# The first projection: 16 blocks by fp32 products from feature rows, 18 blocks whole and wide

## The chip, the cores and the metric

One core of one Trainium2 chip. The kernel is one launch, and its time is device microseconds (us) from start to end; of several runs the median is taken. The engines are named as in the profile: PE (TensorE matmuls), PEld (its weight loads), DVE (VectorE), ACT (ScalarE), POOL (GpSimd), SP (the queue that issues the loads).

## The reference, cut to what matters

Two transformer blocks follow each other on x of 256 tokens by 2048 features, in float32. The change touches only the start of the first:

```python
mod = silu(c) @ w_ada + b_ada                    # w_ada 2048 x 12288
sh_a, sc_a, gt_a, sh_f, sc_f, gt_f = split(mod, 6)
h = rmsnorm(x, norm_mix) * (1.0 + sc_a) + sh_a   # shift: columns 0:2048, scale: 2048:4096 of w_ada
p = h @ w_in                                     # 2048 x 9296
c_q, c_kv, k_pe, q_g, k_g, v_g, z, b_logit, a_logit, gate_logits = split_cols(p)
```

The branches behind p are a latent attention (MLA: c_q, c_kv and k_pe, with an RMS norm on c_q and c_kv), a gated delta rule (q_g, k_g and v_g pass a causal convolution of four taps with silu, then an l2 norm; b_logit and a_logit give its gates), and sigmoid gates. A second block without modulation follows.

## The kernel before, in words

The matrices have features in partitions: h is 16 tiles of 128 features by 256 tokens. A product of 128 features of the input with 128 of the output is a *tile*; there are 6864. Weights come in *units* of 512 KB (128 x 1024, eight tiles). Each unit of a linear layer (kind "L") is split in two: ACT rounds it to fp32r (`hi`, L519), DVE takes the rest (`lo`, L659); h is split likewise (H1). A *narrow* tile is three fp32r products of 256 columns (L354 to L356: hi by hi, hi by lo, lo by hi). A *wide* tile is two: hi by both halves of h in one product of 512 columns, lo by hi in one of 256 (L348 to L352); its bank holds two sums, which ACT and DVE add when they take it out (`raw_sum`, with L523 and L671).

A unit of w_ada (kind "A", 192 of them) is multiplied on DVE by c and added to an accumulator (L651, L655), one unit of 128 rows of c by 1024 columns after the other; after 16 units, PE sums over partitions (`mod_sum`, L361). The first 64 units, four *groups* of 16, give shift and scale for four tiles of h each. So tiles 0 to 3 of h exist after 16 units, 4 to 7 after 32, and so on.

A single function, `walk`, is run once per engine, and fixes the order of the work on each. `kinds` is the order of the units in the load queue; there are 13 slots for them at first (5 RAW, 8 EARLY, the latter in room that H2 takes later), and 5 after unit `early`. Work beside the tiles is put in generators with `later(gen, lag, gap)`: they start `lag` tiles on and give one step every `gap` tiles. `force()` runs one step of each when a bank or result is missing. PSUM's 8 banks are two rings, `lbank` (3) and `mbank` (5).

The first projection has 34 blocks of output (`CBLK`: c_q, c_kv, k_pe and the gate logits b, a; `Q03`, `Q47`: 24 of q, k, v), each over 16 tiles of h, 544 narrow tiles. It runs in four eras: `partial` takes all 34 blocks over tiles 0 to 3 of h, then over 4 to 7, then over 8 to 11, and the last loop (`LATE`) over 12 to 15. What an era leaves is kept in `part` (B1 and B2). ACT copies out the first era; in the second and third, every second block is added by DVE (`combine`, L709) and every second one by ACT and POOL (L523, L932); the last is added by DVE. `kinds` puts 17 L units and 16 A units in each of the first three eras.

Behind and beside the last era come: `cnorm` (the norms of c_q, c_kv), `qkv_chain` (the taps L760, tanh L534 and product L713 of 24 blocks), `l2norm(0)` (eight sums on PE, L403, and four spreads L408), then `ups(0)` to `ups(7)` (the latent attention's up projections, 112 narrow tiles, with the attention of 8 heads in steps beside them), then 16 blocks of gate b, gate a, z, and so on, all wide. `gdn()` (L824 to L872), the delta rule in four rounds, is put up ahead of `ups` and waits for `l2norm(0)`; it gives one step each 4 tiles, beside whatever tiles there are.

Of the kernel before, what the change touches and what calls it, by code (L numbers as in the profile page):

```python
# [12 lines left out]
ERA = 17  # L13
HAND = 4
TAPS = 4
# [178 lines left out]
SIGNALS = ("tile", "hi", "lo", "ada", "mod_p", "mod_v", "pre_a", "pre_v", "ev_a", "ev_v", "ev_g", "ev_p",  # L194
           "st_a", "st_v", "st_g", "st_p", "ad_v", "l2_a", "l2_v", "l2_p", "gd_p", "gd_a", "gd_v", "at_p", "at_a",
           "at_v", "at_g", "cv_a", "cv_v", "cv_p", "spin")
LOADS = tuple(f"raw{i}" for i in range(NRAW + NEARLY)) + tuple(f"bias{i}" for i in range(4)) + ("cols", "consts", "x", "pos", "x2", "out")


def program(nc, xT, pos, cols_d, consts_d, wada, wst, bias_d, out, log):  # L200
# [8 lines left out]
    with ctx:  # L209
# [71 lines left out]
        RQ, RV = SC[:, 0:2], SC[:, 2:4]  # L281
        R12, R1, ACC2 = B3[:, 0, :], B3[:, 1, :], B3[:, 2, :]
# [8 lines left out]
        ACC = (ADA[:, :], B2[:, 20:24, :].rearrange("p a t -> p (a t)"))  # L291
# [8 lines left out]
        def sync(e):  # L300
# [9 lines left out]
            def load_x(i):  # L310
                e.dma_start(X[:, 4 * i:4 * i + 4, :], xT[:, 4 * i:4 * i + 4, :]).then_inc(S["x"], 16)

            def load_x2(i, free):
                q.wait_ge(free)
                e.dma_start(X[:, 4 * i:4 * i + 4, :], xT[:, 4 * i:4 * i + 4, :]).then_inc(S["x2"], 16)
# [24 lines left out]
        def tensor(e):  # L340
            q = Engine(e, S)

            def tile(u, i, bk, H, k, wide, second, first, last, lo, h, free):
# [160 lines left out]
            walk(dict(tile=tile, mod_sum=mod_sum, spin=spin, stat_add=stat_add, stat_sum=stat_sum, acc2_sum=acc2_sum, rope_turn=rope_turn, ba_turn=ba_turn,  # L504
# [5 lines left out]
        def scalar(e):  # L510
            q = Engine(e, S)

            def c_sigmoid(cols):
                q.wait_ge(cols)
                e.activation(SC[:, 16:32], col("c", 0, 16), ACT.Sigmoid).then_inc(S["pre_a"], 1)

# [113 lines left out]
            walk(dict(c_sigmoid=c_sigmoid, hi=hi, copy_sum=copy_sum, split_hi=split_hi, tanh=tanh, sigmoid=sigmoid, square=square,  # L630
# [3 lines left out]
        def vector(e):  # L634
# [13 lines left out]

            def ada_first(acc, slot, raw, c, free):
                q.wait_ge(raw, c, free)  # L650
                e.tensor_scalar(acc, raw_at(slot), SC[:, 0:1], None, mult).then_inc(S["ada"], 1)  # L651
# [12 lines left out]

            def mod_add2(g, bk, summed, cols):
                q.wait_ge(summed, cols)
                e.tensor_tensor(m2h(MOD[:, 0:32])[:, :, 4 * g:4 * g + 4], m2h(bk[:, 0:8]), m2h(col("b_ada", 0, 32))[:, :, 4 * g:4 * g + 4], add).then_inc(S["mod_v"], 1)
# [230 lines left out]
            walk(dict(c_silu=c_silu, halve=halve, norm_product=norm_product, ada_first=ada_first, ada_next=ada_next, lo=lo, mod_add=mod_add, mod_add2=mod_add2, sum_halves=sum_halves,  # L898
# [37 lines left out]
        def walk(mine, log=None):  # L936
            w = Walk(mine)
            do, load, later, need, now = w.do, w.load, w.later, w.need, w.now
            st = {"load": 0, "proc": 0, "na": 0, "nl": 0, "la": 0, "ll": 0}
            tv = Ring(w, [TV[:, i, :] for i in range(4)])  # L940
# [4 lines left out]
            kinds = ["A"] * 16  # L945
            for g in range(GROUPS - 1):
                put = 0
                for i in range(ERA):
                    due = min(16, max(0, -(-16 * (i - 1) // (ERA - 5))))
                    kinds += ["L"] + ["A"] * (due - put)  # L950
                    put = due
            put = 16 * GROUPS
            late_at = len(kinds) - 16
            for i in range(ERA * (GROUPS - 1), N_TILES // 8):
# [3 lines left out]
            lin_at = [i for i, k in enumerate(kinds) if k == "L"]  # L958
            early = 16 * GROUPS + ERA * (GROUPS - 1)
# [5 lines left out]
            group_tok = [None] * GROUPS  # L965
# [5 lines left out]
            def load_next():  # L971
# [5 lines left out]
                if kinds[s] == "A":  # L977
# [15 lines left out]
            def proc_next():  # L993
                s = st["proc"]
                slot = slot_of(s)
                if kinds[s] == "A":
# [3 lines left out]
                    acc = ACC[j % 2] if j < GROUPS else ACC[0]  # L1000
                    if t == 0:
                        before = j - 2 if j < GROUPS else j - 1
# [1400 lines left out]
```

## Time and profile before

| | |
|---|---|
| runs | 2845.52 us median of 3 (2835.41 to 2852.19) |
| the profiled execution | 2841.27 us, span 2839.3 us, mean granted clock 0.989 |
| PE, DVE, ACT, POOL busy | 2723.7, 2033.5, 1359.1, 207.0 us |
| loaded | 560.39 MB read, 199 GB/s on average |

A stage's busy times are read beside its length: the engine that is nearly full there sets it. PE's ends are modelled, so that a matmul of 0.28 us can start 0.12 us after the one before it: what a product costs in a stream is the distance of starts. An fp32 product stands in the profile as two records.

### The profile page before, as it was taken

Reading aid. Unit: us, or ns where it says so; the run is one execution under the profiler, and the core shown is the slowest. Engines: PE = TensorE matmul, PEld = TensorE weight load, DVE = VectorE, ACT = ScalarE, POOL = GpSimd, SP = SyncE. Lnnn points to the kernel's source line nnn. Section 1 sums busy time; section 2 is a strip of 40 time slices with the busy share of each in tenths; the row PEclk is TensorE's granted clock in tenths of the full one; section 3 lists DMA queues with packets and bytes.
Section 4 is the critical chain, followed back from the end, with each engine's and each line's share of the span. In section 5 each row is a group of like instructions: output and inputs, shape, how many; then the busy total and the mean of one; then the engine's idle time right before and its main releaser. Section 6 shows DMA issues by size and latency. Waiting matters only on the chain.

```text
span 2839.3 us, 43991 instructions
## 1 busy us (share of the span) xinstructions
PE 2723.7 (96%) x17404; PEld 2453.9 (86%) x17404; DVE 2033.5 (72%) x2989; ACT 1359.1 (48%) x2169; POOL 207.0 (7%) x180
## 2 busy tenths in 40 slices
PE   6988899999999999999999999999999999999997
PEld 6888888998899788888888889998888888888886
DVE  7898787777796886555555679996567566565665
ACT  4445753433444544444444554466554444444454
POOL 0231000000002000000000180111110000000001
PEclk9999999999999999999999999999999999999999
DMA  9864355566787686555555554544445555555553
GB/s 391 315 234 134 104 179 192 195 213 203 255 304 254 224 301 217 189 189 190 189 188 191 186 173 163 180 166 138 157 134 178 191 187 191 186 190 189 186 192 126
DMA packets 158461, 565.37 MB, mean 199 GB/s; under 512 B 17584, under 2 KB 21936, under 8 KB 158256
## 3 DMA queue, kind: packets, MB, share of 16 engines
q1 hardware_dynamic: 158256, 562.56, 58.4%
q8 instruction: 138, 2.26, 0.3%
q14 instruction: 67, 0.55, 0.1%
HBM read 560.39 MB, written 2.10 MB: 198 GB/s over the span
## 4 chain that ended last, share of the span: by engine, by line
PE 84%; DVE 10%; ACT 3%; issue 2%; DMA 1%; SPq 0%; POOL 0%; DVEq 0%; ACTq 0%; POOLq 0%
PE BK L351 20%; PE BK L349 20%; PE BK L352 10%; PE BK L348 10%; PE BK L354 6%; PE BK L356 5%; PE BK L355 5%; DVE LO L659 3%; PE BK L436 2%; ACT HI L519 1%; DVE ADA L655 1%; DVE B L878 1%; DVE B L709 1%; PE BK L361 1%; DVE TV L760 1%
## 5 line engine op out<-in xcount | busy, mean ns | idle before, releaser
L519 ACT ACTIVATE HI<-RAW 128x1024 fp32r<-128x1024 f32 x825 | 875.0, 1061 | 1229.8 <-PE BK L349 846.8
L659 DVE TENSOR_TENSOR LO<-RAW,HI 128x1024 fp32r<-128x1024 f32 x825 | 1017.0, 1233 | 376.8 <-ACT HI L519 374.4
L351 PE MATMUL BK<-H,HI 128*128 128x512 f32 x2528 | 1011.2, 402 | 8.9 <-DVE LO L659 8.5
L349 PE MATMUL BK<-H,HI 128*128 128x512 f32 x2496 | 985.7, 396 | 0.0
L352 PE MATMUL BK<-H,LO 128*128 128x256 f32 x2528 | 703.0, 278 | 0.0
L348 PE MATMUL BK<-H,LO 128*128 128x256 f32 x2496 | 698.4, 280 | 0.4 <-DVE H L705 0.2
L354 PE MATMUL BK<-H,HI 128*128 128x256 f32 x1840 | 547.8, 298 | 35.2 <-DVE B L709 16.8
L348 PEld LDWEIGHTS BK<-H,LO 128*128 128x128 f32 x2496 | 469.8, 188 | 111.5 <-DVE H L705 2.0
L352 PEld LDWEIGHTS BK<-H,LO 128*128 128x128 f32 x2528 | 477.1, 189 | 100.1 <-issue 0.7
L355 PE MATMUL BK<-H,HI 128*128 128x256 f32 x1840 | 525.8, 286 | 0.0
L356 PE MATMUL BK<-H,LO 128*128 128x256 f32 x1840 | 525.5, 286 | 0.0
L351 PEld LDWEIGHTS BK<-H,HI 128*128 128x128 f32 x2528 | 481.3, 190 | 18.4 <-DVE LO L659 10.0
L349 PEld LDWEIGHTS BK<-H,HI 128*128 128x128 f32 x2496 | 469.3, 188 | 3.8
L354 PEld LDWEIGHTS BK<-H,HI 128*128 128x128 f32 x1840 | 357.6, 194 | 51.8 <-DVE B L709 18.5
L355 PEld LDWEIGHTS BK<-H,HI 128*128 128x128 f32 x1840 | 358.1, 195 | 2.1
L356 PEld LDWEIGHTS BK<-H,LO 128*128 128x128 f32 x1840 | 357.7, 194 | 0.0
L914 POOL TENSOR_TENSOR SQ<-SQ,B 128x256 f32<-128x256 f32 x63 | 81.2, 1288 | 1491.5 <-ACT B L542 1487.8
L655 DVE SCALAR_TENSOR_TENSOR ADA<-RAW,SC,ADA 128x1024 f32<-128x1024 f32 x133 | 171.0, 1286 | 2.8 <-DMA RAW<-wada_dram 1.9
L705 DVE TENSOR_TENSOR H<-TV,H 128x256 fp32r<-128x256 f32 x124 | 52.4, 424 | 165.8 <-ACT H L530 165.6
L671 DVE TENSOR_TENSOR TV<-BK,TE 128x256 f32<-128x256 f32 x255 | 106.2, 418 | 36.9 <-ACT TE L523 36.8
L523 ACT ACTIVATE TE<-BK 128x256 f32<-128x256 f32 x352 | 128.2, 366 | 1.2 <-PE BK L349 0.8
L878 DVE SCALAR_TENSOR_TENSOR B<-B,CO 128x256 f32<-128x256 f32 x240 | 110.3, 520 | 1.8 <-ACT B L602 1.8
(248 smaller groups left out, 1878.8 us busy)
## 6 DMA issues: line engine op xcount, KB each, us to landing
RAW<-wst_dram SPq DMA_DIRECT2D x825, 512.0 KB, 3.3
RAW<-wada_dram SPq DMA_DIRECT2D x155, 512.0 KB, 4.5
EARLY<-wada_dram SPq DMA_DIRECT2D x37, 512.0 KB, 8.9
EARLY<-wst_dram SPq DMA_DIRECT2D x33, 512.0 KB, 7.7
X<-xT_dram SPq DMA_DIRECT2D x8, 512.0 KB, 9.2
B<-bias_dram SPq DMA_DIRECT2D x32, 128.0 KB, 3.3
out_dram<-X SPq DMA_DIRECT2D x3, 512.0 KB, 2.7
CN<-consts_dram SPq DMA_DIRECT2D x1, 900.0 KB, 9.7
```

The costliest lines, as they stand in the source:

```text
L348: e.matmul(bk[:, 256:512], ll, H[:, k, 0:256], start=False, stop=False, skip_group_check=True)
L349: e.matmul(bk[:, :], hh, H[:, k, :], start=False, stop=last, skip_group_check=True).then_inc(S["tile"], 1)
L351: e.matmul(bk[:, :], hh, H[:, k, :], start=first, stop=False, skip_group_check=True)
L352: e.matmul(bk[:, 256:512], ll, H[:, k, 0:256], start=False, stop=last, skip_group_check=True).then_inc(S["tile"], 1)
L354: e.matmul(bk[:, 0:256], hh, H[:, k, 0:256], start=first, stop=False, skip_group_check=True)
L355: e.matmul(bk[:, 0:256], hh, H[:, k, 256:512], start=False, stop=False, skip_group_check=True)
L356: e.matmul(bk[:, 0:256], ll, H[:, k, 0:256], start=False, stop=last, skip_group_check=True).then_inc(S["tile"], 1)
L519: e.activation(HI[:, u % NHL, :], raw_at(slot), ACT.Copy).then_inc(S["hi"], 1)
L523: e.activation(dst, src, ACT.Copy).then_inc(S["ev_a"], 1)
L655: e.scalar_tensor_tensor(acc, raw_at(slot), SC[:, t:t + 1], acc, mult, add).then_inc(S["ada"], 1)
L659: e.tensor_tensor(LO[:, u % NHL, :], raw_at(slot), HI[:, u % NHL, :].bitcast(f32), sub).then_inc(S["lo"], 1)
L878: e.scalar_tensor_tensor(CA[j], UP[:, j, i:i + 256], CO[:, o + i:o + i + 1], CA[j], mult, add).then_inc(S["cv_v"], 1)
```

## The change

The first 64 units of w_ada are laid out the other way round: a unit (kind "R") holds 128 *output features* in partitions by 1024 of the 2048 values of c; four such units (shift and scale, two halves each) are a *feature row*. c is spread to all partitions once (`c_spread`, `c_row`: CR). DVE multiplies the unit by CR in place, ACT sums it over its free axis. After four units shift and scale of one tile of h are there (`mod_row`), and `modulated` makes that tile in float32 (HF, in B2); x is scaled by its norm ahead of that (`x_scaled`). The tile is also split into H1, as before.

The first 16 of the 34 blocks (`FIRST`: CBLK and six of Q03) are accumulated over the 16 rows in all 8 banks, two blocks to a bank, by one fp32 product per tile (`direct`), straight from the loaded unit (kind "D") without hi and lo. The order of loads is R for two rows, then per row two D units and the four R units of the row two on. When row 15 is done, the 16 halves are copied out, and the 18 other blocks (`REST`) run whole over 16 tiles of h as wide tiles. There are no partial sums, no `part_add` on POOL, and no `mod_sum` for these 64 units. `cnorm`, k_pe and the logits are thus put up first; the tap chain starts 24 tiles into REST, at a step each 6 tiles (`TAPS`, 4 before); `scalars` steps each 4 tiles (8 before); `l2norm(0)` starts 64 tiles in. x's squares are four instructions of 1024 columns, each waiting for its own quarter of x, and c and x are loaded ahead of all units.

The core of the diff:

```diff
-ERA = 17
+ROWS_AHEAD = 2
+DIRECT = 16
-TAPS = 4
+TAPS = 6
+            def direct(slot, i, bk, o, k, last, raw, h, free):
+                q.wait_ge(raw, h, free)
+                e.matmul(bk[:, o:o + 256], raw_at(slot)[:, 128 * i:128 * i + 128], HF[k], start=(k == 0 and o == 0), stop=last,
+                         skip_group_check=True).then_inc(S["tile"], 1)
+            def unit_sum(slot, c, product):
+                q.wait_ge(product)
+                e.activation(raw_at(slot), raw_at(slot), ACT.Copy, accum_out=SM[:, c:c + 1]).then_inc(S["ada_a"], 1)
+            def unit_product(slot, half, raw, row):
+                q.wait_ge(raw, row)
+                e.tensor_tensor(raw_at(slot), raw_at(slot), CR[:, 1024 * half:1024 * half + 1024], mult).then_inc(S["ada"], 1)
-            kinds = ["A"] * 16
-            for g in range(GROUPS - 1):
...
+            kinds = ["R"] * (4 * ROWS_AHEAD)
+            for i in range(16):
+                kinds += ["D"] * (DIRECT // 8) + ["R"] * (4 if i + ROWS_AHEAD < 16 else 0)
...
+            spin(10)
+            def row_end(j, sums):
+                x = do("x_scaled", "ad_v", j, rs_tok[0], tk_x[j // 4])
+                m = do("mod_row", "mod_v", j, sums, tk_cols, n=3)
+                yield
+                hf_tok[j] = do("modulated", "ev_a", j, m, x)
+                yield
+                h_tok[j] = yield from split(H1, j, HF[j], hf_tok[j])
+                row_done.pop(0)
...
-            for k in range(0, 12, 4):
-                partial(range(k, k + 4))
...
+            for r in range(16):
+                if r + ROWS_AHEAD < 16 + 1 and r > 0:
+                    for i in range(4):
+                        row_unit(r + 1, i)
+                while hf_tok[r] is None:
+                    next(row_done[0], None)
+                direct_row(r)
...
-            later(scalars(), 16, 8)
-            later(l2norm(0), 0, 6)
-            later(qkv_chain(), 0, TAPS)
+            for b, n in enumerate(FIRST):
+                own, bk, _ = held[b // 2]
+                later(ev_first(n)(bk[:, 256 * (b % 2):256 * (b % 2) + 256], done_tok[b | 1], (own, b % 2)))
+            later(scalars(), 16, 4)
+            later(l2norm(0), 64, 6)
+            later(qkv_chain(), 24, TAPS)
+            for n in REST:
+                run(block(H1, h_tok, 0, "w_in", 0, n, ev_qkv(n - 9, True), wide=True))
```

`row_unit(j, i)` is the product and the sum of one unit, and a step of the last row's `row_end`; `direct_row(r)` is 16 `direct` tiles from two units.

## Rows read from the trace of the kernel before

**Rows 1.** the page: busy time per engine over the span

```profile
PE 2723.7 (96%) x17404; PEld 2453.9 (86%) x17404; DVE 2033.5 (72%) x2989; ACT 1359.1 (48%) x2169; POOL 207.0 (7%) x180
```

**Rows 2.** windows by stage: length, busy per engine (instructions), clock, DMA share, GB/s

```profile
39.90:100.00 60.10, 58.73 (x443) 55.38 (x444) 46.16 (x50) 30.12 (x57) 0.00 (x0) 0.97 0.90 351
100.00:200.00 100.00, 88.90 (x701) 85.87 (x699) 95.02 (x109) 39.47 (x61) 37.26 (x28) 0.98 0.84 305
200.00:240.00 40.00, 35.46 (x278) 34.51 (x278) 30.42 (x51) 22.10 (x37) 12.69 (x12) 0.97 0.28 93
240.00:287.00 47.00, 40.73 (x300) 37.18 (x300) 42.20 (x91) 26.51 (x45) 0.00 (x0) 0.99 0.40 132
287.00:358.50 71.50, 62.71 (x455) 58.59 (x455) 56.28 (x127) 52.87 (x139) 0.00 (x0) 0.98 0.30 99
...
378.00:450.00 72.00, 70.52 (x452) 62.97 (x451) 58.66 (x80) 32.98 (x56) 0.00 (x0) 1.00 0.59 198
```

**Rows 3.** the timeline to the first tile: start us, us, engine, line

```profile
17.28 9.80 PE L366 MATMUL BK<-TE,CN 128*128 128x256 f32 x32 [17.28 <-ACT TE L542]
...
39.89 0.55 PE L354 MATMUL BK<-H,HI 128*128 128x256 f32 x1 [2.13 <-DVE H L701]
```

**Rows 4.** two narrow tiles in steady running, the timeline

```profile
43.69 0.28 PE L354 MATMUL BK<-H,HI 128*128 128x256 f32 x1
...
44.05 0.28 PE L354 MATMUL BK<-H,HI 128*128 128x256 f32 x1
```

**Rows 5.** one pair of wide tiles and the next, the timeline of PE

```profile
1600.13 0.40 PE L351 MATMUL BK<-H,HI 128*128 128x512 f32 x1
...
1600.83 0.39 PE L351 MATMUL BK<-H,HI 128*128 128x512 f32 x1
```

**Rows 6.** the chain of work: start us, us, line, count

```profile
83.00 1.68 PE BK L361 x16
...
420.33 0.86 PE BK L408 x4
```

**Rows 7.** groups of instructions by form, from 0 to 520 us

```profile
L659 DVE TENSOR_TENSOR LO<-RAW,HI 128x1024 fp32r<-128x1024 f32 x85 | 107.9, 1271 | 5.8 <-ACT HI L519 5.8
L519 ACT ACTIVATE HI<-RAW 128x1024 fp32r<-128x1024 f32 x85 | 89.9, 1058 | 134.7 <-PE BK L349 74.3 <-PE BK L356 54.1 <-DMA RAW<-wst_dram 4.3
...
L932 POOL TENSOR_TENSOR B<-B,TE 128x256 f32<-128x256 f32 x34 | 43.7, 1286 | 176.2 <-ACT TE L523 176.2
...
L709 DVE TENSOR_TENSOR B<-BK,B 128x256 f32<-128x256 f32 x60 | 24.8, 415 | 0.0
```

**Rows 8.** the timeline of DVE, tap chain beside the last era

```profile
268.32 1.22 DVE L659 TENSOR_TENSOR LO<-RAW,HI 128x1024 fp32r<-128x1024 f32 x1
...
269.79 1.51 DVE L760 SCALAR_TENSOR_TENSOR TV<-B,CO,TV 128x255 f32<-128x255 f32 x3
...
271.79 0.43 DVE L713 SCALAR_TENSOR_TENSOR B<-B,TV 128x256 f32<-128x256 f32 x1
272.13 1.22 DVE L659 TENSOR_TENSOR LO<-RAW,HI 128x1024 fp32r<-128x1024 f32 x1
...
286.44 0.42 DVE L709 TENSOR_TENSOR B<-BK,B 128x256 f32<-128x256 f32 x1
```

**Rows 9.** the timeline of DVE while POOL adds

```profile
105.54 1.75 DVE L659 TENSOR_TENSOR LO<-RAW,HI 128x1024 fp32r<-128x1024 f32 x1
```

**Rows 10.** windows: two stretches of the first loads

```profile
0.00:20.00 20.00, 2.72 (x7) 2.18 (x7) 7.91 (x11) 3.36 (x7) 0.19 (x4) 1.00 0.91 346
...
60.00:80.00 20.00, 19.42 (x151) 18.20 (x151) 17.55 (x15) 9.71 (x19) 0.00 (x0) 1.00 1.02 407
```

**Rows 11.** lines 760 and 828 (first of gdn): durations, first and last start

```profile
L760 DVE SCALAR_TENSOR_TENSOR TV<-B,CO,TV x72: 466/482/486, 262.0 to 376.4; 128x255 f32<-128x255 f32 x24, 128x254 f32<-128x254 f32 x24, 128x253 f32<-128x253 f32 x24
...
L828 DVE TENSOR_TENSOR B<-CN,B x4: 628/656/685, 378.3 to 636.7; 128x512 f32<-128x512 f32 x4
```

**Rows 12.** the timeline of ACT: an activation with a sum read out

```profile
298.80 0.19 ACT L584 ACTIVATION_READ_ACCUMULATOR B<-B,SC 128x1 f32 x1
```

More of the change, by code:

```diff
@@ new lines, in walk, with row_unit @@
+            spin(10)
+            row_done = []
+            hf_tok = [None] * 16
+            def row_unit(j, i):
+                s, slot = st["proc"], slot_of(st["proc"])
+                v = do("unit_product", "ada", slot, i % 2, raw(s), cr_tok)
+                raw_free[slot] = do("unit_sum", "ada_a", slot, 4 * j + i, v)
+                st["proc"] += 1
+                while load_next():
+                    pass
+                for f in list(row_done):
+                    next(f, None)
+                if i == 3:
+                    row_done.append(row_end(j, raw_free[slot]))
@@ L1213, in rotary @@
                     yield
-                for _ in range(16):
+                for _ in range(7):
                     yield
@@ new lines, in walk, with __init__, release @@
+            REST = (CBLK + Q03 + Q47)[DIRECT:]
+            later(rotary(), 8, 8)
+            class Halves:
+                def __init__(self, ring, i):
+                    self.ring, self.i, self.used = ring, i, []
+                def release(self, half, *signals):
+                    self.used.append(list(signals))
+                    if len(self.used) == 2:
+                        self.ring.release(self.i, *self.used)
+            held = []
+            for b in range(DIRECT // 2):
+                ring = lbank if lbank.idle else mbank
+                bi, bk, fr = ring.get()
+                held.append((Halves(ring, bi), bk, fr))
@@ new lines, in walk, with direct_row @@
+            hi_tok.update({u: None for u in range(2 * DIRECT)})
+            done_tok = [None] * DIRECT
+            def direct_row(r):
+                for g in range(DIRECT // 8):
+                    s = lin_at[w.tile // 8]
+                    slot = slot_of(s)
+                    for i in range(8):
+                        b = 8 * g + i
+                        own, bk, fr = held[b // 2]
+                        w.tile += 1
+                        if log is not None:
+                            log.append(("w_in", r, FIRST[b]))
+                        done_tok[b] = do("direct", "tile", slot, i, bk, 256 * (b % 2), r, r == 15, raw(s), need(hf_tok, r), fr if r == 0 else None)
+                    raw_free[slot] = done_tok[b]
+                    assert st["proc"] == s
+                    st["proc"] += 1
+                    while load_next():
+                        pass
+                    w.flush()
@@ new lines, in walk @@
+            for r in range(16):
+                if r + ROWS_AHEAD < 16 + 1 and r > 0:
+                    for i in range(4):
+                        row_unit(r + 1, i)
+                while hf_tok[r] is None:
+                    next(row_done[0], None)
+                direct_row(r)
+            while row_done:
+                next(row_done[0], None)
+            r_last = ("ada", w.count["ada"])
+            p1_end = [("tile", w.tile), h_tok[15], r_last]
+            feed(w.tile // 8 + 2)
@@ L1284, in f @@
                 def f(bk, tok, own):
-                    half, hk = half_of(j)
-                    cq_tok[j] = combine(CQ[j], bk, half, add, tok, own, hk, x_used)
+                    cq_tok[j] = copy_out(CQ[j], bk, tok, own, x_used)
                     yield
+                    while j > 3 and SQS[0].done is None:
+                        yield
                     if j == 4:
-                        while SQS[0].done is None:
-                            w.force()
                         SQS[1] = Stats(*SQS[0].before, SQS[0].done)
```

186 lines of the change are left out of this document (78 added, 108 removed).

## The prediction

> **What bounds the kernel now.** The page comes first: PE is busy 96% of the span, DVE 72% [rows 1]. So time can be won only where PE idles or where its work shrinks. The windows by stage show where it idles. Its first tile starts at 39.9 us [rows 3]. From there to 287 us, the end of the first projection (DVE takes its last sum out at 286.4 [rows 8]), PE is busy 223.8 of 247.1 us, and then 62.7 of the 71.5 us of the `ups` [rows 2]. From 378 us on it is nearly full (70.5 of 72). Busy time hides part of it, since each matmul's modelled end runs past the next start. Counted by starts, a narrow tile takes 0.36 us [rows 4], and 544 of them 196 us. With some 8 us of sums beside them (three `mod_sum` at 1.68 us [rows 6] and small things), 204 us of work take 247: 43 us are lost, after 40 us of start.
>
> What fills the other engines there: DVE is busy 95 of the 100 us from 100 to 200, and 42.2 of 47 from 240 to 287 [rows 2]. In the second and third era a `lo` takes 1.75 us while POOL adds [rows 9], against a mean of 1.27 and 1.22 alone [rows 7, 8]. In the last era the period is 3.81 us (from `lo` to `lo` [rows 8]) for eight narrow tiles, 2.9 us of PE: DVE sets the pace, with a `lo`, two sums and one block's taps.
>
> **The start.** Before, c and one group of 16 units must be there ahead of the first tile. After, c, x (2.1 MB) and eight units are needed, with two chains. x's quarters land by about 9 us; c's spread is 16 short fp32 products and four copies, to about 13 us. The 16 sums of squares took 9.8 us [rows 3], so norms are ready at about 22 to 24 us. Row 0 then needs two units' products of row 1 on DVE in front of `modulated` on ACT (the queues are in order), some 4 us. I put the first `direct` tile at 28.5 us (25 to 35).
>
> **The direct stage, 16 rows.** PE: an fp32 product of 256 columns with a new stationary each time took 0.43 us (two products, 0.86 for four records [rows 6]). A row of 16 is 6.9 us, 16 rows 110 us, where the same 256 tiles cost 92 us as narrow ones: the change adds 18 us of PE work here. Loads: six units of 0.524 MB per row at 407 GB/s [rows 10] are 7.7 us. DVE: four products like a `lo` without POOL, whose starts lie 1.14 us apart behind it, about 4.6 us, and some 1.2 us of small steps. ACT: four copies of 1.06 [rows 7] with a sum read out (0.19 more [rows 12]), about 5 us, and two steps on a tile of h, 0.8. So loads set the pace at 7.7 us a row, and PE follows at 90%. By 20 us 6.9 MB are in (346 GB/s [rows 10]); the first unit of row 13 ends the first 48.2 MB, at 20 + 41.3/0.407 = 121 us. Behind it come one D unit of row 13, four R units of row 15 and four D units, all in by 133 us, so that rows 13 to 15 go nearly at PE's pace: 121 + 3 x 6.9 = 142 us. By PE alone it would be 28.5 + 110 = 138.5. I take 143, with the change of banks (two ACT copies ahead of the first bank, mostly while row 15 still runs).
>
> The Trainium skill (FP8 and Floating Point Precision, TensorE Precision Notes) says true fp32 takes four passes, against the three products of a narrow tile. By that rule a tile would be 4/3 of 0.36, an estimate of 0.48 us, 123 us in all, and PE as slow as the loads. The row shows 0.43, so the trace is a little kinder, and the sum uses the row.
>
> **The wide stage.** A pair of wide tiles takes 0.70 us [rows 5], so 288 tiles are 100.8 us. Beside them PE has `l2norm(0)`: 8 row sums at 0.43 and four spreads at 0.86, 6.9 us, by the same row of 0.86 [rows 6], and about 2.5 us for norms, k_pe and logits. DVE: 36 `lo` at 1.14 (41 us), 22 blocks of taps, tanh and product at 1.77 by starts (1.43 and 0.34; 39 us), 18 sums of halves at about 0.34 (6 us), norms, rotary, scalars, l2 rows about 17 us (an estimate: some 45 steps of 0.3 to 0.45 us, by the starts of L709 and L713 [rows 8]): 103 of 110 us. That is tight but does not bind alone: 12 tiles a block of taps are 4.2 us of PE, against 3.75 of DVE. At the front 16 copies, eight squares, tables and splits crowd on ACT beside `hi`; HI and LO hold three units, 8.4 us. For this crowd and the tight stretch I allow 10 us of stalls (4 to 20). The end is 143 + 101 + 9.4 + 10 = 263 us, against 287: 24 us won.
>
> **Behind it.** `l2norm(0)` lay behind 287 before, since the taps ran to 376.4 [rows 11]; now it is done: 6.9 us of PE work less. DVE loses 17 of 24 blocks of taps there (17 x 1.77 = 30 us), and ACT their two passes each. But `gdn`, whose first decay step stood at 378.3 [rows 11], can start with the `ups`, and brings its own DVE steps and in-order waits. The work of `gdn` isn't smaller, only earlier. Of the 8.8 us in which PE idles there [rows 2] I take half as won: 4 us (0 to 9, or a loss of 10 if it crowds). The hundreds of us after are full for PE before, and I take nothing from them.
>
> The first 64 units cost DVE the same (1.2 us each by either operation), the D units cost neither `hi` nor `lo`, and `part_add` leaves POOL: nothing on the path beyond what is counted. The angles for k_pe run in the direct stage, where DVE has 1.9 us free a row. SP issues in order and waits for slots: 13 slots are 2 rows ahead, 15 us, and a D unit is freed at most 7 us after it is used, so no wait binds unless PE falls behind.
>
> The sum: 24 + 6.9 + 4 = 35 us. Against the profiled execution's own time, 2841.3, that gives 2806; it lies 4 us below the median of the runs shown, so against 2845.5 the figure is 2810. Between them I give **2809**.
>
> **Rivals.**
> *The delta rule crowds the attention (0.17).* Both want `mbank`, DVE and PE in order. For it: in the `ups` DVE had 56.3 and ACT 52.9 of 71.5 us [rows 2], and PE waits there for single softmax steps. Against it: 30 us of taps go. If each of some 28 steps costs PE 0.6 us, 17 us are lost: gain 18, 2827 us.
> *DVE or ACT paces the wide stage (0.10).* If the tap chain runs at 5 us a block rather than 4.2, 22 blocks cost 17 us: 2827 too. For it: 3.81 us periods in the last era came with only 90% busy DVE [rows 2, 8].
> *Loads slower than 407 GB/s in the direct stage (0.04).* At 358 the 41.3 MB take 115 us and not 101, 14 us more: 2823. Against it stand the 20 us windows at 407 [rows 10]. The Trainium skill (DMA: Bandwidth & Descriptors, Specifications) gives a limit of about 358 GB/s per core from HBM; by that rule the time is this rival's, but the trace disagrees, with 407.
> *More is won (0.09).* If both stages stall less (3 us) and the `ups` win all 9, and later waits for the delta rule's end shrink by 5: gain 52, 2794.
> *Slower (0.08).* PE's clock falls to 1.2 GHz in the direct stage, where each row leaves PE waiting for loads. Then a product is 0.86 us and a row 13.8; 16 rows are 220 us and the kernel about 80 us slower than forecast, 2885. It decides from 35 / 0.43 = 81 products, about five rows of 16, at the lower level. Against it: with waits in every 8 tiles from 100 to 200 us, PE kept 0.98 of the clock [rows 2].
> *The forecast itself (0.52):* first direct tile 25 to 32, its end 138 to 148, wide stage 113 to 125 long, gain 26 to 44.
>
> **How the numbers follow.** Own range of the likeliest: 2800 to 2819. The range takes in the losses of rivals one to three and half of "more": 2790 to 2834; outside lie 0.08 slower, a few hundredths of the crowding cases together, and the best ones. A change of 0.5% (14 us) is about what a measurement tells from none. Faster by over that: 0.52 + 0.09 + three quarters of 0.31 (18 us hardly clears 14) = 0.84, less a little for causes not thought of: 0.80. Same: 0.11. Slower: 0.09.
>
> **What the profile after would show.** Right: POOL almost empty before 150 us; `direct` about 0.43 us a start, rows 7.7 us apart, 400 GB/s until about 130 us; the last at 140 to 148; no narrow tile until about 263; wide pairs 0.70 us apart with `lo` never late; gdn's first L828-like step within 15 us of the first `ups`. Wrong: a granted clock under 0.9 between 30 and 145; direct products more than 0.5 us apart; ACT in front of `hi` for more than 8 us behind the direct stage; PE busy below 85% in the `ups`. The sum fails most easily in the wide stage's stalls and in what the `ups` give back.

## The result, and the profile after

The kernel after takes 2826.69 us (median of 7 runs, 2822.4 to 2828.04), the kernel before 2845.52 (7 runs, 2835.41 to 2852.19): a ratio of 0.9936, 95% interval 0.9923 to 0.9948. That is 18.8 us faster, about half of the 36 us forecast. The profiled execution took 2822.49 us with a span of 2820.7.

The page, busy time per engine over the span. Against [rows 1] POOL lost 48 us, DVE 60, PE only 3:

```profile
PE 2720.4 (96%) x16824; PEld 2429.0 (86%) x16824; DVE 1973.0 (70%) x2951; ACT 1387.3 (49%) x2235; POOL 158.7 (6%) x146
```

The timeline of PE in the direct stage: start, length, line, and in brackets the idle time before and what ended it. This answers to [rows 3] and to the pace in [rows 2]:

```profile
25.66 9.85 PE L364 MATMUL BK<-B,EARLY 128*128 128x256 f32 x32 [5.04 <-ACT B L538]
35.35 7.07 PE L364 MATMUL BK<-B,RAW 128*128 128x256 f32 x32
...
102.99 7.17 PE L364 MATMUL BK<-B,RAW 128*128 128x256 f32 x32 [0.51 <-DMA RAW<-wst_dram]
110.67 7.17 PE L364 MATMUL BK<-B,EARLY 128*128 128x256 f32 x32 [0.51 <-DMA EARLY<-wst_dram]
118.35 7.17 PE L364 MATMUL BK<-B,RAW 128*128 128x256 f32 x32 [0.51 <-DMA RAW<-wst_dram]
126.31 7.17 PE L364 MATMUL BK<-B,EARLY 128*128 128x256 f32 x32 [0.78 <-DMA EARLY<-wst_dram]
133.99 1.35 PE L364 MATMUL BK<-B,RAW 128*128 128x256 f32 x5 [0.51 <-DMA RAW<-wst_dram]
```

A row is 32 records, 16 products. Without a wait the next row starts 6.91 us on (35.35 to 42.26), 0.43 us a product; with the wait for the load it is 7.68 (102.99 to 110.67 to 118.35). Both are the forecast's numbers. The first row shows the lower clock (0.50 from 26 to 30 us), 9.7 us for 16 products. That seems to cost nothing later, since from 95 us on every row waits for its load.

Windows by stage: start and end, length, busy time of PE, PEld, DVE, ACT and POOL with instructions, PE's clock, DMA share, GB/s:

```profile
30.00:125.00 95.00, 90.77 (x406) 77.87 (x405) 74.20 (x121) 65.05 (x124) 0.00 (x0) 0.98 1.03 409
...
148.00:180.00 32.00, 21.85 (x109) 17.96 (x107) 18.70 (x44) 21.32 (x45) 5.19 (x6) 0.84 0.33 115
180.00:220.00 40.00, 37.92 (x214) 32.61 (x215) 36.80 (x66) 24.05 (x44) 0.00 (x0) 1.00 0.56 182
220.00:250.00 30.00, 28.76 (x160) 24.64 (x158) 23.23 (x40) 21.08 (x39) 0.00 (x0) 1.00 0.47 157
250.00:276.00 26.00, 25.34 (x142) 22.17 (x143) 23.46 (x44) 12.61 (x21) 0.00 (x0) 1.00 0.48 149
276.00:365.00 89.00, 79.74 (x616) 75.19 (x615) 54.66 (x110) 44.36 (x115) 0.00 (x0) 0.98 0.30 96
```

The hole is in one place: of the 32 us from 148 on PE is busy 21.85, at 0.84 of the clock. Three markers tell where the gain lies. The first narrow tile (the end of the first projection) starts at 275.8 us, against 286.8 before: 11.0 won of the 24 forecast. The reload of x, far behind, is issued at 767.2 against 784.1: 17.0 won, so 5.9 between the markers, where 6.9 + 4 were forecast. The span is 18.6 shorter, so 1.6 came behind. The last two are small beside what the same kernel varies by: run again (e0 below), it took 493.0 us between the markers where the run here took 491.3 (before: 497.3), and 2055.4 behind the reload where the run here took 2053.5 (before: 2055.2). So 4 to 6 us were won between the markers, and nothing that can be told from none behind them.

What PE waited for from 147.7 to 275.8 (line, releaser: us in total, times, longest):

```profile
PE BK L413 <- DVE B L816: 8.5, 1, 8.5
PE BK L355 <- DVE LO L703: 2.3, 3, 0.9
PE BK L385 <- POOL SQ L954: 1.4, 2, 1.2
PE BK L423 <- DVE RS L765: 1.3, 1, 1.3
PE BK L418 <- ACT TE L603: 0.6, 1, 0.6
```

14.1 us, of which 8.5 is a single wait: PE's queue holds the gates' running sum (L413, two tiny products), which needs DVE's L816. Why L816 is late stands in the timelines of ACT and of DVE:

```profile
156.68 1.04 ACT L542 ACTIVATE HI<-RAW 128x1024 fp32r<-128x1024 f32 x1
...
160.52 0.42 ACT L553 ACTIVATE H<-TV 128x256 fp32r<-128x256 f32 x1 [1.73 <-DVE TV L753]
161.83 0.42 ACT L553 ACTIVATE H<-TV 128x256 fp32r<-128x256 f32 x1 [0.89 <-DVE TV L753]
...
164.44 0.42 ACT L553 ACTIVATE H<-TV 128x256 fp32r<-128x256 f32 x1 [0.89 <-DVE TV L753]
164.87 1.28 ACT L572 ACT_TABLE_LOAD   x1
166.16 1.28 ACT L586 ACT_TABLE_LOAD   x1
...
167.69 1.28 ACT L589 ACT_TABLE_LOAD   x1
...
169.45 1.04 ACT L542 ACTIVATE HI<-RAW 128x1024 fp32r<-128x1024 f32 x1
```

```profile
161.32 0.48 DVE L753 SCALAR_TENSOR_TENSOR TV<-X,CO,RS 128x256 f32<-128x256 f32 x1
162.28 0.43 DVE L745 TENSOR_TENSOR H<-TV,H 128x256 fp32r<-128x256 f32 x1 [0.48 <-ACT H L553]
162.62 0.48 DVE L753 SCALAR_TENSOR_TENSOR TV<-X,CO,RS 128x256 f32<-128x256 f32 x1
...
169.78 0.17 DVE L816 SCALAR_TENSOR_TENSOR B<-B 128x16 f32<-128x16 f32 x1
```

`cnorm(1)` needs the last piece of `cnorm(0)` (`need(H2_tok, 3)`), and so all four pieces are issued in one burst. Each goes DVE, ACT, DVE (L753, L553, L745) with a wait at each hand-over, 1.30 us a piece; behind them ACT loads three tables. After the `hi` (L542) that starts at 156.68 the next starts at 169.45, 12.8 us on.

PE behind that wait:

```profile
170.01 0.61 PE L413 MATMUL BK<-B,CN 128*128 128x16 f32 x2 [8.47 <-DVE B L816]
...
171.89 0.63 PE L353 MATMUL BK<-H,HI 128*128 128x512 f32 x1
...
173.17 0.63 PE L353 MATMUL BK<-H,HI 128*128 128x512 f32 x1
...
175.18 0.40 PE L353 MATMUL BK<-H,HI 128*128 128x512 f32 x1
...
175.87 0.40 PE L353 MATMUL BK<-H,HI 128*128 128x512 f32 x1
```

A pair of wide tiles takes 1.28 us until about 174.5 (the level of 1.2 GHz) and 0.69 to 0.70 from then on: some 1.6 us more.

### The profile page after: what moved, and what is told of

The parts are those of the page before. It is cut to its first block, busy times and chain, and to the rows that moved or that the text cites. A ratio compares the mean times of both kernels' runs of the same rounds, so it can differ in the third digit from the quotient of the medians.

```text
span 2820.7 us, 42647 instructions
## 1 busy us (share of the span) xinstructions
PE 2720.4 (96%) x16824; PEld 2429.0 (86%) x16824; DVE 1973.0 (70%) x2951; ACT 1387.3 (49%) x2235; POOL 158.7 (6%) x146
## 4 chain that ended last, share of the span: by engine, by line
PE 83%; DVE 9%; ACT 4%; DMA 2%; issue 1%; SPq 0%; POOL 0%; ACTq 0%; DVEq 0%
PE BK L355 21%; PE BK L353 21%; PE BK L356 10%; PE BK L352 10%; PE BK L358 4%; PE BK L360 4%; PE BK L359 4%; DVE LO L703 2%; PE BK L451 2%; DVE B L918 2%; PE BK L364 2%; ACT HI L542 1%; DMA RAW<-wst_dram 1%; DMA RAW<-wada_dram 1%; PE BK L376 0%
## 5 line engine op out<-in xcount | busy, mean ns | idle before, releaser
L542 ACT ACTIVATE HI<-RAW 128x1024 fp32r<-128x1024 f32 x826 | 875.6, 1060 | 1202.2 <-PE BK L353 828.6
L355 PE MATMUL BK<-H,HI 128*128 128x512 f32 x2672 | 1070.0, 402 | 12.2 <-DVE LO L703 11.6
L353 PE MATMUL BK<-H,HI 128*128 128x512 f32 x2640 | 1042.1, 396 | 0.0
L356 PE MATMUL BK<-H,LO 128*128 128x256 f32 x2672 | 743.2, 278 | 0.0
L352 PE MATMUL BK<-H,LO 128*128 128x256 f32 x2640 | 738.3, 280 | 0.4 <-DVE H L745 0.2
L352 PEld LDWEIGHTS BK<-H,LO 128*128 128x128 f32 x2640 | 496.7, 188 | 118.2 <-DVE H L745 2.0
L356 PEld LDWEIGHTS BK<-H,LO 128*128 128x128 f32 x2672 | 504.0, 189 | 106.5 <-issue 0.7
L355 PEld LDWEIGHTS BK<-H,HI 128*128 128x128 f32 x2672 | 508.1, 190 | 23.6 <-DVE LO L703 14.9
L353 PEld LDWEIGHTS BK<-H,HI 128*128 128x128 f32 x2640 | 496.0, 188 | 3.7
L358 PE MATMUL BK<-H,HI 128*128 128x256 f32 x1296 | 383.5, 296 | 13.9 <-DVE LO L703 7.8
L359 PE MATMUL BK<-H,HI 128*128 128x256 f32 x1296 | 368.1, 284 | 0.0
L360 PE MATMUL BK<-H,LO 128*128 128x256 f32 x1296 | 368.1, 284 | 0.0
L358 PEld LDWEIGHTS BK<-H,HI 128*128 128x128 f32 x1296 | 249.7, 193 | 20.5 <-DVE LO L703 12.9
L359 PEld LDWEIGHTS BK<-H,HI 128*128 128x128 f32 x1296 | 249.8, 193 | 2.3 <-issue 0.2
L360 PEld LDWEIGHTS BK<-H,LO 128*128 128x128 f32 x1296 | 249.6, 193 | 0.0
L745 DVE TENSOR_TENSOR H<-TV,H 128x256 fp32r<-128x256 f32 x124 | 52.3, 424 | 164.2 <-ACT H L553 164.2
L699 DVE SCALAR_TENSOR_TENSOR ADA<-RAW,SC,ADA 128x1024 f32<-128x1024 f32 x120 | 154.0, 1283 | 0.8 <-DMA RAW<-wada_dram 0.6
L546 ACT ACTIVATE TE<-BK 128x256 f32<-128x256 f32 x336 | 122.1, 366 | 1.2 <-PE BK L353 0.8
## 6 DMA issues: line engine op xcount, KB each, us to landing
B<-bias_dram SPq DMA_DIRECT2D x32, 128.0 KB, 3.3
```

Of the source, the lines that this page charges most:

```text
L352: e.matmul(bk[:, 256:512], ll, H[:, k, 0:256], start=False, stop=False, skip_group_check=True)
L353: e.matmul(bk[:, :], hh, H[:, k, :], start=False, stop=last, skip_group_check=True).then_inc(S["tile"], 1)
L355: e.matmul(bk[:, :], hh, H[:, k, :], start=first, stop=False, skip_group_check=True)
L356: e.matmul(bk[:, 256:512], ll, H[:, k, 0:256], start=False, stop=last, skip_group_check=True).then_inc(S["tile"], 1)
L542: e.activation(HI[:, u % NHL, :], raw_at(slot), ACT.Copy).then_inc(S["hi"], 1)
L546: e.activation(dst, src, ACT.Copy).then_inc(S["ev_a"], 1)
```

## The experiments

All ran beside the kernel before on the same chip; "stage" is the length of the wide stage in the profiled run, from its first tile to the first narrow tile; "T1" is the start of that narrow tile, and "reload" the issue of x's reload. The stage is the steadier measure: the direct stage ends between 147.5 and 149.5 us from run to run (141.1 in e8), and T1 carries that along. Where nothing in the stage was changed (the kernel after, e0, e3, e8) it is 128.0 or 128.1 us, in e7 and e11 126.3 and 125.6, in e12 and e16 105.1 twice.

| kernel | us, median | ratio (95%) | stage | T1 | reload |
|---|---|---|---|---|---|
| e0 the kernel after again | 2826.72 | 0.9944 (0.9928 to 0.996) | 128.0 | 277.4 | 770.5 |
| e1 scalars 16, 8 | 2825.76 | 0.9943 (0.9928 to 0.9959) | 128.1 | 276.0 | 769.8 |
| e2 scalars 64, 8 | 2823.99 | 0.9941 (0.9927 to 0.9954) | 129.7 | 278.2 | 768.1 |
| e4 TAPS 4 | 2829.86 | 0.9962 (0.9947 to 0.9977) | 134.7 | 282.2 | 771.3 |
| e5 the old order of side work | 2845.51 | 1.0013 (1.0004 to 1.0022) | 146.4 | 294.6 | 787.6 |
| e6 norm's pieces spread | 2822.7 | 0.9931 (0.9918 to 0.9945) | 125.6 | 274.6 | 766.3 |
| e7 e6 and scalars 64, 8 | 2822.43 | 0.993 (0.9918 to 0.9942) | 126.3 | 274.8 | 764.4 |
| e8 less to load | 2818.89 | 0.9917 (0.9899 to 0.9935) | 128.0 | 269.0 | 759.5 |
| e3 gdn at `ups(6)` | 2821.07 | 0.9925 (0.9908 to 0.9941) | 128.0 | 276.4 | 764.1 |
| e9 chain from tile 0 | 2827.65 | 0.9946 (0.9927 to 0.9965) | 132.1 | 280.2 | 769.3 |
| e10 e7, chain behind the stage | 2816.5 | 0.9914 (0.9891 to 0.9937) | 104.4 | 252.7 | 759.3 |
| e11 e7 and e3 | 2817.43 | 0.9911 (0.9895 to 0.9928) | 125.6 | 274.3 | 760.5 |
| e12 e10, chain from tile 96 | 2807.36 | 0.9874 (0.9856 to 0.9892) | 105.1 | 252.8 | 747.6 |
| e13 e7, chain from tile 64 | 2808.58 | 0.9884 (0.9866 to 0.9902) | 116.4 | 264.4 | 751.2 |
| e14 e9 and TAPS 4 | 2842.18 | 1.0002 (0.9992 to 1.0011) | 143.6 | 291.3 | 783.8 |
| e15 chain from tile 96 alone | 2824.55 | 0.9938 (0.9924 to 0.9951) | 119.8 | 267.8 | 767.7 |
| e16 e12 and e3 | 2807.86 | 0.9878 (0.9864 to 0.9892) | 105.1 | 253.6 | 750.8 |
| e17 e6, chain from tile 96 | 2819.59 | 0.9925 (0.9911 to 0.9938) | 112.5 | 260.3 | 763.7 |

**Is it one wait? (e1, e2)**

```diff
-            later(scalars(), 16, 4)
+            later(scalars(), 16, 8)    # e1; 64, 8 in e2
```

> The steps of the gates' scalars 8 tiles apart instead of 4 (as in the kernel before), nothing else. Theory A (PE stands still because the cumulating matmul is put up ahead of its inputs: the DVE and ACT queues are still busy with the norms): the matmul comes 12 tiles, 4.2 us, later in PE's order, so the wait shrinks from 8.5 to 4 to 5 us, with less time at the lower clock behind it; 4 to 6 us faster than e0. Rival B (DVE and ACT are the bound of this stretch, PE's wait is only where it shows): the wait moves to the weights' lo and the time stays within 1.5 us of e0.

> The scalars start 64 tiles into the wide stage instead of 16, 8 tiles a step. Theory A: the 8.5 us wait and the 1.8 us at the lower clock behind it go whole, 9 to 11 us faster than e0, less up to 2 us for two or three more activation table loads of 1.28 us in the tap chain. Rival B: within 2 us of e0, with waits for lo in its place.

The same view of PE's waits, of e1 (first two lines) and of e2 (last two), each from 147.7 to 276 us:

```profile
PE BK L413 <- DVE B L816: 5.6, 1, 5.6
PE BK L355 <- DVE LO L703: 3.6, 1, 3.6
```

```profile
PE BK L355 <- DVE LO L703: 7.3, 4, 3.5
PE BK L413 <- DVE B L816: 3.0, 1, 3.0
```

8.5 + 2.3 became 5.6 + 3.6, and then 3.0 + 7.3. The wait for the gates goes to `lo`, and the stage stays (128.1 and 129.7 us, against 128.0 in e0); the kernel is 1.0 and 2.7 us from e0, near what rival B expects. With the matmul moved away, the burst still keeps ACT from `hi`. "An early matmul in PE's queue" falls as the cause: it is only where PE notices.

**The gap of the chain, and the old order (e4, e5, e9, e14)**

```diff
-TAPS = 6
+TAPS = 4                           # e4, e5, e14
-            later(scalars(), 16, 4)
-            later(l2norm(0), 64, 6)
-            later(qkv_chain(), 24, TAPS)
+            later(scalars(), 16, 8)            # e5
+            later(l2norm(0), 0, 6)             # e5
+            later(qkv_chain(), 0, TAPS)        # e5, e9, e14
```

> The tap chain gives a step each 4 tiles instead of 6; it ends some 100 tiles earlier. If DVE has the room that I worked out (3.75 us of work for each 4.2 us of PE), it has not at this pace: 1.0 lo, one block's taps and half a sum in 2.8 us of PE is 3.1 us of DVE, so the wide stage is 5 to 10 us longer for two thirds of its length and then shorter, the sum within 4 us of e0. Rival (the pace of the taps sets the delta rule's start): faster by 3 us or more, with the delta rule's first step before 276 us.

> The order of the side work as the kernel before has it (taps at once and each 4 tiles, l2 norm at once, scalars each 8 tiles), on the new scheme. Theory: the taps then share DVE and ACT with the norms from the first tile, the start of the wide stage is worse; the first narrow tile comes at 280 to 290 us instead of 276, and the whole is 3 to 10 us slower than the changed kernel. Rival (the order behind the direct stage doesn't matter, only the work does): within 2 us.

> The kernel after, with the tap chain started at the first wide tile instead of 24 tiles in (one number; gap of 6 kept). The kernel with the whole old order of side work took 2845.5 and its wide stage ended 19 us later. Theory 'tanh passes between the norms' passes: each change between tanh and another table costs ACT 1.28 us, and DVE's in-order queue waits for ACT, so that lo is late': the chain's start is most of it; ACT loads 12 or more tables up to the end of the stage (7 in the kernel after), lo is waited for by 10 us or more, the first narrow tile at 284 to 292, kernel 2835 to 2842. Rival 'the gap of the chain (4 against 6) is most of it': the first narrow tile at 276 to 281, kernel 2827 to 2831.

> The kernel after with the chain at the first wide tile and a gap of 4 (the two together; each alone moved the first narrow tile by 4 to 6 us, and with the old places of scalars and l2norm(0) too it was 19). If the two just add: first narrow tile 286, kernel 2832 to 2836. If it is the two together that make the 19 us: 292 to 296, kernel 2840 to 2846.

e5 missed by far: with the old order the new direct stage is worth nothing (2845.5, T1 294.6). e4 came in as expected. e9 did not bear its theory out: T1 and the whole time lie in its rival's ranges, and PE waits once, 12.8 us, for L816, and not for `lo`. e14 lies near the second of its two cases. Alone, the gap makes the stage 6.6 us longer and the chain's start 4.0; together 15.5 (e14). So they don't add. From 147 to 276 us ACT loads 7 tables in the kernel after, 11 in e9, 12 in e14 and 14 in e5, each 1.28 us: tanh and the norms' functions take turns. But their number does not set the stage's length: e4 loads 7 in 134.7 us, e6 and e7 below load 10 and 11 in 125.6 and 126.3. In e5 DVE waits longest for one tanh, with five table loads ahead of it on ACT between 176.9 and 185.2 us:

```profile
185.60 0.43 DVE L753 SCALAR_TENSOR_TENSOR B<-B,TV 128x256 f32<-128x256 f32 x1 [6.15 <-ACT B L557]
185.94 1.22 DVE L703 TENSOR_TENSOR LO<-RAW,HI 128x1024 fp32r<-128x1024 f32 x1
```

The `lo` behind it in DVE's queue comes late. PE's two long waits lie on either side: 9.2 us until 177.2, for the `lo` before this one, which stood behind the norm's four pieces, a block of taps and a tanh; and 6.6 us until 189.3, for L816.

**Spread the burst (e6, e7)**

```diff
             def cnorm(half):
...
+                while half and H2_tok[3] is None:
+                    yield
```

> The norm of c_kv waits with a yield for the norm of c_q instead of forcing its steps. Theory C: that force puts the eight steps of c_q's norm (DVE, ACT, DVE, four times 1.3 us) in one burst in front of hi and lo, 158 to 166 us, and the three units of split weights run dry; spread out, ACT and DVE reach hi again after one step, the wait of the cumulating matmul shrinks to under 4 us, and the first narrow tile comes 4 to 8 us earlier. Rival (the table loads and the gates' own chain, not the burst, set it): first narrow tile within 2 us of 276.

> The same wait with a yield, and the scalars 64 tiles in, 8 tiles a step. Theory C: neither burst nor early matmul; PE waits under 4 us between 150 and 200 us, first narrow tile at 264 to 268 us, the whole 8 to 12 us faster than the changed kernel. Rival (DVE's share of the wide stage is the bound, 102 of 128 us with its round trips): at best 3 us faster.

The clock from 148 to 180 us is 1.00 in both, where it was 0.84, and PE is busy 27.4 and 29.6 of these 32 us, not 21.9. But the next 40 us pay for it (35.4 and 32.2, not 37.9), where taps, norms and scalars meet: the stage is 2.5 and 1.8 us shorter. The kernel is 4 us faster than e0, but its ratio (0.9931, 0.993) is within the interval of the kernel after's (0.9923 to 0.9948), so a gain in the whole time isn't shown. Both expectations missed: T1 was to come 4 us earlier or more. PE's waits in e7:

```profile
PE BK L413 <- DVE B L816: 6.0, 1, 6.0
PE BK L355 <- DVE LO L703: 3.9, 5, 1.8
PE BK L423 <- DVE RS L765: 1.3, 1, 1.3
```

**Take the chain away (e10), bring it back later (e12, e13, e15, e17)**

```diff
-            later(l2norm(0), 64, 6)
-            later(qkv_chain(), 24, TAPS)
+            later(l2norm(0), 320, 6)           # e10, e12
+            later(qkv_chain(), 288, TAPS)      # e10; 96 in e12, e15, e17; 64 in e13
```

e10, e12 and e13 stand on e7, e17 on e6, e15 on the kernel after.

> From the kernel with the norm's waits and late scalars (2822.4): the tap chain starts 288 tiles into the wide blocks, behind all of them, and the l2 norm's sums 320 tiles in, so that the wide stage has no taps, no tanh and no l2 norm. Theory 'DVE's and ACT's side steps in order set the wide stage': with 22 blocks of taps (39 us of DVE) gone, lo is never late behind the norms, the 7 us of l2norm(0) on PE are gone too, and the first narrow tile is at 275 - 7 - 6 = 262 (258 to 265). Rival 'the front alone (norms, scalars) holds the stage up': 267 to 269, by the l2 norm's 7 us alone. The kernel as a whole: the taps go beside the ups and the delta rule starts late, so that its end (hg_done) may be waited for: 2822 to 2850; I say 2835.

> The kernel with the taps behind the wide stage (2816.5, first narrow tile at 252.7), with the chain started 96 tiles into the wide blocks, so that 16 of its 24 blocks lie in the wide stage, but none beside the norms and the scalars. Theory 'it is the chain beside the norms and scalars that costs, not the chain': the wide stage stays within 3 us of 252.7 (252 to 256), and with 16 blocks of taps gone from the ups the kernel takes 2806 to 2815. Rival 'each block of taps beside wide tiles costs PE 0.8 us or so': first narrow tile at 264 to 268, kernel 2816 to 2822.

> The kernel with the norm's waits and late scalars (2822.4, first narrow tile 274.8), with one number changed: the chain starts 64 tiles in, not 24. The scalars still start at 64, so the two overlap. By the theory that the overlap with the norms and scalars costs, the part of it that lies with the norms goes: first narrow tile at 262 to 268, kernel 2812 to 2818. By the rival (taps cost wherever they lie): 1 to 3 us won by the blocks that leave the stage, 2819 to 2822.

> The kernel after with one number changed: the tap chain starts 96 tiles into the wide blocks, not 24 (norms, scalars and l2norm(0) as in the kernel after). If what failed in my sum was the chain beside the norms and scalars, this alone makes most of the missing gain: the low clock and the long wait ahead of the gates' sums go or shrink, first narrow tile at 258 to 266 (with up to 7 us of l2norm(0) in it), kernel 2806 to 2813. Rival (the norm's waits and the scalars' late place are needed too): first narrow tile 268 or later, kernel 2816 or more.

> The kernel with the norm's waits alone (2822.7, first narrow tile 274.6) with the tap chain started 96 tiles in: the two edits together, and nothing else. Each alone was worth 2 to 4 us; the kernel with both, with late scalars and a late l2norm(0), was worth 19. If the long burst of norms and the chain are two causes of which either one holds the wide stage up, both gone give what their sum does not: first narrow tile 253 to 261 (some 3 us of it l2norm(0)), kernel 2806 to 2813. If the late scalars or the late l2norm(0) are needed: first narrow tile at 264 or later, kernel 2815 to 2823.

With no taps in it, the wide stage takes 104.4 us (e10) for 100.8 us of tiles. T1 (252.7) and the whole time (2816.5) came in below all that was expected of e10. With 16 blocks of taps in it, but none beside the norms, it takes 105.1 (e12). So the taps cost PE 0.7 us at most where they lie behind the norms. e12 came in as expected; e13's T1 did too, and its whole time was 3 us better than its range. e13 and e7 differ by one number, the chain's start (64 against 24): the stage is 9.9 us shorter and the kernel 13 to 14 us faster, the clearest single step of all. PE's waits in e12 up to T1 are 1.4 us in all, and its windows are full at the whole clock:

```profile
PE BK L385 <- POOL SQ L954: 0.7, 1, 0.7
PE BK L413 <- DVE B L816: 0.5, 1, 0.5
PE BK L355 <- DVE LO L703: 0.2, 1, 0.2
```

```profile
148.00:180.00 32.00, 31.32 (x178) 26.92 (x177) 21.50 (x39) 23.33 (x42) 5.05 (x6) 1.00 0.59 198
180.00:220.00 40.00, 39.24 (x225) 33.72 (x224) 35.26 (x66) 25.87 (x49) 0.00 (x0) 1.00 0.53 173
220.00:253.00 33.00, 33.00 (x192) 28.78 (x191) 30.01 (x51) 19.55 (x34) 0.00 (x0) 1.00 0.59 191
```

ACT in e12 puts a `hi` between the norm's pieces, where the kernel after had none for 12.8 us:

```profile
158.51 1.05 ACT L542 ACTIVATE HI<-RAW 128x1024 fp32r<-128x1024 f32 x1
161.29 0.42 ACT L553 ACTIVATE H<-TV 128x256 fp32r<-128x256 f32 x1 [1.73 <-DVE TV L753]
161.61 1.05 ACT L542 ACTIVATE HI<-RAW 128x1024 fp32r<-128x1024 f32 x1
163.49 0.42 ACT L553 ACTIVATE H<-TV 128x256 fp32r<-128x256 f32 x1 [0.83 <-DVE TV L753]
...
164.07 1.05 ACT L542 ACTIVATE HI<-RAW 128x1024 fp32r<-128x1024 f32 x1
```

To compare stages, the part of `l2norm(0)`'s 6.9 us of PE work that lies in them is taken off (all in the kernel after, e6 and e13, half in e15 and e17, whose spreads come behind T1, none in e12): 121.2 us for the kernel after, 118.7 for the spread norm (e6), 116.4 for the late chain (e15), 109.1 for both (e17), 105.1 for both with the scalars and `l2norm(0)` late (e12). The single edits win 2.5 and 4.8, the two together 12.1. There are two causes, and each hides part of the other. What the late scalars and the late `l2norm(0)` win on top (4.0) was not taken apart.

e15 and e17 missed in the whole time (2806 to 2813 was expected of both); e15's lies in its rival's range. T1 of e17 came in as expected, but from T1 to the reload it takes 503 us, where e12 takes 495 and e13 487 (3.4 of `l2norm(0)` lie in e17's, 6.9 in e12's). So its ratio, 0.9925, is hardly told from the kernel after's. In both, the delta rule starts beside the `ups` while the taps still run (L868 from 284.5, L800 until 324.5 in e17); in e12 the taps end at 301.1 and L868 starts at 335.9. But in e13 they lie beside each other too (267.0 and 302.4) and cost nothing like it.

**The delta rule's place (e3, e11, e16)**

```diff
-            later(gdn(), 0, HAND)
             for h in range(8):
+                if h == 6:
+                    later(gdn(), 0, HAND)
                 ups(h)
```

> The kernel after, with the delta rule put up ahead of ups(6) instead of ahead of ups(0). It tells whether the delta rule beside the latent attention costs or gives time. Theory 'waits follow the work' (the 4 us that I had from the ups are given back to the delta rule's own waits): the ups get shorter (89 to about 76 us for the 112 tiles), the tiles behind them get longer, and the time from the first narrow tile to the reload of x stays within 3 us of 491; the kernel within 4 us of the kernel after (2826.7), ratio 0.992 to 0.995. Rival 'it crowds': 10 to 17 us are won, 2812. Rival 'an early start is what helps': 6 us or more are lost, since the delta rule's end is waited for later, 2833 or more.

> The kernel with the norm's waits and late scalars (2822.4), with the delta rule put up ahead of ups(6) as well. If the two edits add up and the delta rule's place is worth nothing: 2822 plus or minus 3. If the delta rule crowds the attention: 2808 to 2812.

> The best kernel so far (chain at 96, norm's waits, late scalars and l2norm(0): 2807.4) with the delta rule put up ahead of ups(6). There the delta rule already starts 83 us behind the first narrow tile (335.9), where ups(6) comes at about 320, so I expect no difference: 2804 to 2810. If it wins 5 us again, as it did twice from the kernels with an early chain, 2802.

Put up behind six of the eight `ups`, it makes the kernel 5.6 and 5.0 us faster (from e0 and from e7; by the ratios 5.4 both times), and the stretch from T1 to the reload 5.3 us (e0) and 3.4 us (e7) shorter. Both lie between the two theories of e3 and e11. The 112 narrow tiles of the `ups` take 70 us in e3 and 90 in e0, so starting it early does crowd the attention, but 14 of those 20 us come back behind it. From e12, where it starts that late anyway, it does nothing, as expected.

**The loads (e8)**

```diff
+                if u < 2 * DIRECT and u >= 8:
+                    e.dma_start(raw_at(slot)[:, 0:256], wst[u][:, 0:256]).then_inc(S[f"raw{slot}"], 16)
+                    return
```

24 of the 32 D units load only their first quarter; the 16 blocks of p are computed from what the slots hold.

> From the fifth row of the direct stage on, a D unit loads only its first quarter; the products read what stands in the slot, so p's first 16 blocks are wrong, and everything else is done. Theory (loads set the row, 7.7 us): rows go at PE's pace, 6.9 us apart, and the last direct product starts near 140 us instead of 147.7, so the whole is 6 to 8 us faster. Rival (the chain product, sum, modulated, or the wait for slots sets the row): rows stay at 7.5 us or more.

The window from 30 to 125 us, which was 90.77 of 95 for PE at 409 GB/s:

```profile
30.00:125.00 95.00, 93.47 (x429) 80.83 (x428) 79.92 (x131) 70.46 (x136) 0.00 (x0) 1.00 0.94 356
```

With loads off the path, rows lie 6.9 us apart from 99.75 on, the wide stage starts 6.6 us earlier than in the kernel after (8.4 than in e0), T1 comes 6.8 us earlier, and the kernel is some 8 us faster (two runs; by the ratio 5 to 8), as expected. What is won in the direct stage is kept to the end, and some 7 us are all that its loads cost.

## Why the prediction was wrong, and where it was right

Right, step by step:
- The start: 28.5 was forecast (25 to 35), and it was 25.66.
- The direct stage's costs: 0.43 us a product, rows 7.68 us apart, 409 GB/s. The rivals "loads slower than 407 GB/s" and "PE's clock falls" are out: from 30 to 125 us PE had 0.98 of the clock. The Trainium skill's limit of about 358 GB/s for a core (DMA: Bandwidth & Descriptors, Specifications) would have made a row 8.8 us, an estimate from that figure; the measured rate, 409, decides.
- The tiles of the wide stage: 0.70 us a pair, and 104.4 us for the stage where nothing crowds it (e10).
- That the two places where the sum "fails most easily" were the wide stage's stalls and the `ups`.

Wrong:
- **"For this crowd and the tight stretch I allow 10 us of stalls (4 to 20)."** This term of the sum failed. It was 17.9: the stage took 128.1 us, less 100.8 and 9.4 (e0: 128.0), and so it was longer than the 113 to 125 that the forecast itself allowed. The views show 14.1 of waits and 1.6 of low clock; 2.2 are left over, in gaps that no view names. The text even named it ("ACT in front of `hi` for more than 8 us behind the direct stage"), and it was 12.8. I counted DVE's and ACT's busy time and found it tight but enough. That holds (DVE was busy 102 of 128 us). What binds is the hand-over between two in-order queues: four pieces of a norm at 1.30 us each, tables at 1.28, with `hi` or `lo` queued behind. The rival "DVE or ACT paces the wide stage" comes nearest: its condition was a block of taps each 5 us, and from 171.73 to 272.03 the 22 blocks start 4.78 us apart, of which 0.3 is `l2norm(0)`. It blamed the pace of the whole chain; e12 shows the same gap of 6 at no cost behind the norms, so what failed is its meeting with them.
- **"143" for the end of the direct stage.** It was 147.7, 4.7 late. The count of bytes to row 13's first unit was too low, and so row 13 started at 126.3, not at 121: by then 50.2 MB had been moved, not 48.2. The 87 units and x are 47.7; columns, constants and positions are another 1.5, of which the count has 0.5 at most. The other 1 MB was not traced.
- **"Of the 8.8 us in which PE idles there I take half as won: 4 us."** Between T1 and the reload 5.9 us were won (4.3 in e0), less than `l2norm(0)`'s own 6.9, so the `ups` gave nothing. The delta rule took it (e3, e11: 3 to 5 us). That is the rival "the delta rule crowds the attention" in its direction, at a third or less of its 17 us. Its time, 2827, was met by another road.

Together: 4.7 for the direct end, 7.9 for the stalls and 5.0 behind T1 are 17.6 of the 18 us missing; roundings make the rest. The forecast's own 2809 is what e12 and e13 measure: the gain was there, and the order of side work withheld it. But that they meet the number is partly luck. In e12 the direct stage still ends 4.7 us late, and the wide stage, with the 6.9 us of `l2norm(0)` added, is 112.0 us, 8 less than forecast.

Two of the prediction's side sums don't come out, and neither enters the forecast. At 0.86 us a product the direct stage would end at 28.5 + 220 = 248.5, 105 us behind 143, and not the "about 80" of the rival "Slower". And if 22 of 24 blocks of taps lie in the wide stage, 15 leave the `ups`, not 17.

Shown by runs: that the burst and the early chain are two causes that hide part of each other; that the direct stage's loads are worth some 7 us; that the delta rule's early start costs 3 to 5. Not shown: that table loads, more than DVE's time, make the chain costly at the front. Their number goes with the stage in e9, e14 and e5, but not in e4, e6 and e7, and no run took them away alone. Open: why T1 to the reload is 16 us longer in e17 than in e13 (3.4 of it are spreads of `l2norm(0)`). PE waits 22.1 us there against 16.0, and from 260 to 300 its clock is 0.91; which meeting of taps, scalars, `l2norm(0)` and delta rule makes it was not isolated.

## What to carry to other kernels

When a stage is rebuilt, the side work's start tiles and gaps must be set again: here they were worth as much as the rebuilt stage itself (2845.5 with the old ones, 2826.7 with the new ones, 2807.4 with better ones). None of these orders was tried on the kernel before, so how much of it that kernel could have won by itself is open. Price side work that goes back and forth between two in-order engines by its hand-overs and by the tables in front of it, not by its busy time; and ask which weight conversion is queued behind it. If removing one wait only makes another, don't conclude that the waits don't matter: remove two candidates at once before dropping either.

## What the runs showed of the hardware

- Two table loads in a row start 1.29 us apart, and the activation behind a load starts at its end (164.87, 166.16, then 167.45): a change of tables cost 1.28 us and nothing beside it in these rows.
- One core read 409 GB/s over 95 us.
- After an idle time of 8.47 us PE ran at the level of 1.2 GHz for some 4 us (a pair of wide tiles in 1.28 us), and was back at 0.70 us from 174.5 on. The length of the idle time alone doesn't tell. In e6, where the idle time there was 2.41 us, the clock from 148 to 180 us was 1.00; but in the direct stage of the kernel after, 2.28 us of waiting for a load until 72.33 were followed by the lower level:

```profile
72.00:74.00 2.00, 1.67 (x4) 1.41 (x5) 1.22 (x3) 2.00 (x5) 0.00 (x0) 0.53 1.03 410
74.00:76.00 2.00, 2.00 (x7) 1.59 (x7) 1.90 (x5) 0.41 (x2) 0.00 (x0) 0.62 1.03 410
```
